# A block's decay gates: tanh quotient to exponential, and its mask rows from VectorE to ScalarE

## The reference, cut to what matters

```python
# LRU: r, i from the convolved input xc, per channel
r = sigmoid(einsum(xb, wr) + br);  i = sigmoid(einsum(xb, wi) + bi)
log_a = -8.0 * r * softplus(-lam)
a = exp(log_a)
mult = sqrt(-expm1(2.0 * log_a))
bx = mult * i * xc
h[t] = a[t] * h[t-1] + bx[t]          # associative scan over time
return h * gelu(u_y)
# SSD, per head: a causal 256x256 mask of exp(cumulated decay differences) times C B^T, applied to x * dt
```

## Time and profile before

| | us |
|---|---|
| median of 3 runs | 2155.76 (2155.23 to 2159.41) |
| span of the profiled execution (the page gives no other time of it) | 2165.0 |
| busy in that span: PE / DVE / ACT / POOL | 1581.4 / 754.1 / 575.8 / 613.3 |
| the head loop, from the first `ssd_y` to the first matmul of the LRU's output layer | 1424.46 to 1507.34 |

### The profile page before, as it was taken

How to read it: one execution, slowest core, us unless ns; L and a number is a source line. 1 busy time by engine, 2 the same in 40 slices (tenths; PEclk the granted TensorE clock), 3 DMA queues, 4 the chain that set the end, 5 groups by cost and what they waited for, 6 DMA issues and landing times.

```text
span 2165.0 us, 25359 instructions
## 1 busy us (share of the span) xinstructions
PE 1581.4 (73%) x10341; PEld 1063.6 (49%) x10341; DVE 754.1 (35%) x989; ACT 575.8 (27%) x973; POOL 613.3 (28%) x252
## 2 busy tenths in 40 slices
PE   4969786665555656666556669687879787889897
PEld 2758642111111111111111259676769777878797
DVE  3225420000000000000000079889739885176333
ACT  4324420000000000000000044553644344444453
POOL 1144300000000000000000049543738556755473
PEclk8989877778888778777887779899979888998898
DMA  9455569999999999999999925222424333443330
GB/s 390 144 192 227 233 241 417 418 419 418 417 417 417 417 417 417 418 419 419 418 417 417 420 89 186 102 102 79 156 78 165 146 117 114 159 146 107 117 117 20
DMA packets 88740, 570.06 MB, mean 263 GB/s; under 512 B 4576, under 2 KB 10720, under 8 KB 44512
## 3 DMA queue, kind: packets, MB, share of 16 engines
q1 hardware_dynamic: 81440, 556.81, 64.2%
q10 hardware_dynamic: 7232, 12.29, 2.1%
HBM read 564.89 MB, written 4.19 MB: 263 GB/s over the span
## 4 chain that ended last, share of the span: by engine, by line
DMA 38%; PE 29%; DVE 25%; ACT 3%; issue 2%; DVEq 1%; another core or an unknown queue 1%; ACTq 0%; POOL 0%; SPq 0%
PE bank L1376 28%; DMA ring<-in_w_down 13%; DMA ring<-in_w_up 12%; DMA ring<-in_w_gate 12%; DVE work L157 4%; DVE work L810 4%; DVE work L806 3%; DVE work L155 1%; DMA ring<-in_dense 1%; ACT work L1692 1%; DVE work L728 1%; DMA ring<-in_w_ada 1%; DVE rstd L1928 1%; DVE work L1932 1%; ACT weights_high_rounded L1692 1%
## 5 line engine op out<-in xcount | busy, mean ns | idle before, releaser
L1357 POOL TENSOR_TENSOR ring_rounded<-ring,weights_high_rounded 128x1024 fp32r<-128x1024 f32 x244 | 608.2, 2505 | 1507.9 <-ACT weights_high_rounded L1692 1507.2
L1376 PE MATMUL bank<-ring,work 128*32 128x512 f32 x3008 | 490.7, 785 | 335.6 <-DMA ring<-in_w_up 129.8
L1692 ACT ACTIVATE work<-bank 128x256 f32<-128x256 f32 (+3 forms) x312 | 135.6, 441 | 1218.1 <-PE bank L1376 863.7
L1376 PEld LDWEIGHTS bank<-ring,work 128*32 128x32 f32 x3008 | 93.8, 127 | 698.7 <-DMA ring<-in_w_up 212.1
L1692 ACT ACTIVATE weights_high_rounded<-ring 128x1024 fp32r<-128x1024 f32 x244 | 255.9, 1052 | 34.1 <-PE bank L1376 22.1
L1376 PE MATMUL bank<-h_high_rounded,weights_high_rounded 128*128 128x256 f32 x1296 | 208.1, 302 | 56.6 <-ACT weights_high_rounded L1692 38.0
L2140 DVE TENSOR_TENSOR work<-work,bank 128x512 f32<-128x512 f32 x16 | 11.0, 688 | 602.4 <-PE bank L1376 602.4
L1376 PEld LDWEIGHTS bank<-h_high_rounded,weights_high_rounded 128*128 128x128 f32 x1296 | 177.7, 199 | 76.3 <-issue 40.7
L1376 PE MATMUL bank<-h_normed_rounded,weights_high_rounded 128*128 128x256 f32 x1296 | 186.7, 289 | 0.0
L1376 PE MATMUL bank<-h_high_rounded,ring_rounded 128*128 128x256 f32 x1296 | 182.4, 285 | 2.7 <-POOL ring_rounded L1357 2.7
L1376 PE MATMUL bank<-work_rounded,weights_high_rounded 128*128 128x256 f32 x1088 | 162.2, 300 | 29.0 <-ACT work_rounded L1692 20.3
(11 more groups left out here) (230 smaller groups left out, 1363.2 us busy)
## 6 DMA issues: line engine op xcount, KB each, us to landing
ring<-in_w_down SPq DMA_DIRECT2D x64, 2048.0 KB, 16.8
ring<-in_w_gate SPq DMA_DIRECT2D x63, 2048.0 KB, 16.6
ring<-in_w_up SPq DMA_DIRECT2D x61, 2048.0 KB, 16.5
ring<-in_dense SPq DMA_DIRECT2D x60, 2048.0 KB, 7.7
ring<-in_w_ada SPq DMA_DIRECT2D x12, 2048.0 KB, 20.5
work<-in_w_up SPq DMA_DIRECT2D x3, 1024.0 KB, 13.6
bias_diagonals<-work ACTq DMA_DIRECT2D x2, 1532.0 KB
ring<-in_dense SPq DMA_DIRECT2D x2, 1024.0 KB, 18.8
```

The lines of the kernel that those rows point to most:

```text
L1357: nc.gpsimd.tensor_tensor(as_r(w), w, w_high[:, buffer, :], ALU.subtract).then_inc(s.w_low, 1)
L1376: return nc.tensor.matmul(o, lhsT, rhs, start=start, stop=stop)
L1692: return nc.scalar.activation(o, i, f, **kw)
```

## The change: an exponential for the LRU's decay, mask rows on ACT

1. The decay a is no longer (1 + tanh) / (1 - tanh). ACT writes Tanh into `XC` (free once i * xc is made) and then Exp into `TH`, with the factor -8 in the new `LAMT`. `lru_input` is gone from DVE; `lru_scan` multiplies by (1 + a) in the instruction that added 1 before. Sqrt takes its minus sign from the activation's scale, so DVE's L737 is gone.
2. The eight products i * xc are made on DVE while the sigmoids come out, each after its own `ri_sig`, and ACT waits for all of them before Tanh.
3. The masked decay rows are written by ACT (`Identity` with a per-partition scale), three before the loop and then one in each head between `weight_high` and `decay(h+2)`. `LMASK` has three buffers; the third is the old `LRU_T`.

```diff
@@ tensor_block2
-                bank, lm = B[4 + h % 2], LMASK[:, h % 2, :]
+                bank, lm = B[4 + h % 2], LMASK[h % 3]
@@ scalar_block2
+            def mask_decay(h):
+                if h >= 3:
+                    act.wait_ge(s.bc_mm, h - 2)
+                fn(LMASK[h % 3], LCUM, ACT.Identity, scale=con("head_rows")[:, h:h + 1]).then_inc(s.lmask_ready, 1)
...
             act.wait_ge(s.ri_sig, KT)
+            act.wait_ge(s.cs_ready, 1)
+            mask_decay(0), mask_decay(1), mask_decay(2)
+            act.wait_ge(s.ixc_ready, 1)
             for k in range(KT):
-                last = fn(TH[:, k, :], TH[:, k, :], ACT.Tanh, scale=LAMC[:, k:k + 1])
+                fn(XC[:, k, :], TH[:, k, :], ACT.Tanh, scale=LAMC[:, k:k + 1])
+            for k in range(KT):
+                last = fn(TH[:, k, :], TH[:, k, :], ACT.Exp, scale=LAMT[:, k:k + 1])
             last.then_inc(s.th_ready, 1)
...
-            act.wait_ge(s.lru_neg, 1)
-            fn(tiles(0, 8), tiles(0, 8), ACT.Sqrt).then_inc(s.lru_root, 1)
+            act.wait_ge(s.th_ready, 1)
+            fn(tiles(0, 8), tiles(0, 8), ACT.Sqrt, scale=-1.0).then_inc(s.lru_root, 1)
...
                     copy2(38 + h, RAW[:, 38 + h, :])
+                if h + 3 < SSM_H:
+                    mask_decay(h + 3)
                 if h + 2 < SSM_H:
                     decay(h + 2)
@@ vector_block2
+            v.tensor_scalar(LAMT, LAMC, -8.0, None, ALU.mult)
             v.tensor_scalar(LAMC, LAMC, -4.0, None, ALU.mult).then_inc(s.lam_ready, 1)
+
+            for k in range(KT):
+                i = tiles(I_OF[k], 1)
+                dve.wait_ge(s.ri_sig, k + 1)
+                last = v.tensor_tensor(i, i, XC[:, k, :], ALU.mult)
+            last.then_inc(s.ixc_ready, 1)
...
-            for h in range(2):
-                v.tensor_scalar(LMASK[:, h, :], LCUM, con("head_rows")[:, h:h + 1], None, ALU.mult).then_inc(s.lmask_ready, 1)
...
-                link(v.scalar_tensor_tensor(out=th, in0=th, scalar=1.0, in1=LRU_T, op0=ALU.add, op1=ALU.mult))
+                link(v.scalar_tensor_tensor(out=i, in0=th, scalar=1.0, in1=i, op0=ALU.add, op1=ALU.mult))
...
-            dve.wait_ge(s.th_ready, 1)
-            dve.wait_ge(s.ri_sig, KT)
-            for k in range(KT):
-                i = tiles(I_OF[k], 1)
-                last = v.tensor_tensor(i, i, XC[:, k, :], ALU.mult)
-            link(last)
-            v.tensor_scalar(tiles(0, 8), tiles(13, 8), -4.0, None, ALU.mult).then_inc(s.lru_neg, 1)
             segments(0)
-            mask_decay(2)
             segments(1)
...
                 if h + 2 < SSM_H:
                     segments(h + 2)
-                if h + 3 < SSM_H:
-                    mask_decay(h + 3)
-                if h % 2 == 0:
-                    lru_input(h // 2)
-                else:
+                if h % 2:
                     lru_scan(h // 2).then_inc(s.act_full, 1)
```

More of the change, by code:

```diff
@@ L95 @@
 lmask_ready seg_ready bc_mm xdt_ready m_ready ya_pair ssd_y ya_sq ya_sum w_high x_ready dt_in dt_soft xbc_conv
-lam_ready th_ready ly_gelu lru_neg lru_root seg_exp z_silu g_sig ya_gated ya_inv ya_rstd conv_step ffn_gelu
+lam_ready ixc_ready th_ready ly_gelu lru_root seg_exp z_silu g_sig ya_gated ya_inv ya_rstd conv_step ffn_gelu
 act_full act_high a_exp late_in lam_soft act_low bias_in lg_sb lg_mm lg_ready pt_sb pt_tr ao_mm gl_mm kp_ready
@@ L331, in program @@
         SEG = [tiles(71, 3)[:, 0:3 * P], tiles(71, 3)[:, 3 * P:6 * P], tiles(61, 2)[:, 0:3 * P]]
-        LMASK = tiles3(74, 2)
+        LMASK = [tiles(74, 1), tiles(75, 1), tiles(12, 1)]
         I_OF = (8, 9, 10, 11, 76, 77, 78, 79)
@@ L335, in program @@
         DTT = small(112, 32).rearrange("p (t h) -> p t h", t=TT)
-        LRU_T = tiles(12, 1)
         PA, PB, MO2 = tiles3(29, 8), tiles3(21, 8), tiles3(13, 8)
@@ L699, in segments @@
                                 ALU.subtract, ALU.min).then_inc(s.seg_ready, 1)
[L701 to L706, removed]
             def lru_scan(k):
@@ L711, in lru_scan @@
                 if k == 0:
+                    dve.wait_ge(s.th_ready, 1)
                     dve.wait_ge(s.lru_root, 1)
                     dve.wait_ge(s.ly_gelu, 1)
-                link(v.scalar_tensor_tensor(out=th, in0=th, scalar=1.0, in1=LRU_T, op0=ALU.add, op1=ALU.mult))
+                link(v.scalar_tensor_tensor(out=i, in0=th, scalar=1.0, in1=i, op0=ALU.add, op1=ALU.mult))
                 link(v.tensor_tensor(i, i, XC[:, k, :], ALU.mult))
@@ L723, in pair_out @@
                                        in1=B[6 + n % 2][:, 0:SEQ], op0=ALU.mult, op1=ALU.add).then_inc(s.ya_pair, 1)
-            def mask_decay(h):
-                dve.wait_ge(s.bc_mm, h - 1)
-                v.tensor_scalar(LMASK[:, h % 2, :], LCUM, con("head_rows")[:, h:h + 1], None, ALU.mult).then_inc(s.lmask_ready, 1)
-            dve.wait_ge(s.th_ready, 1)
-            dve.wait_ge(s.ri_sig, KT)
-            for k in range(KT):
-                i = tiles(I_OF[k], 1)
-                last = v.tensor_tensor(i, i, XC[:, k, :], ALU.mult)
-            link(last)
-            v.tensor_scalar(tiles(0, 8), tiles(13, 8), -4.0, None, ALU.mult).then_inc(s.lru_neg, 1)
             segments(0)
-            mask_decay(2)
             segments(1)
```

## The result

| | before | after |
|---|---|---|
| median of 4 runs each, us | 2155.49 (2153.04 to 2159.41) | 2173.28 (2172.02 to 2175.21) |
| span of the profiled execution, us | 2165.0 | 2170.2 |

The ratio is 1.0086, 95% interval 1.0070 to 1.0103: slower. The forecast was 2174.8 us.

A forecast was written before the change was run, and what follows sets the result against it. It took DVE, held by POOL through their shared port, to bound the head loop, with PE waiting for its product. Terms +3.8, +2.5, -1.3, +15.0 and -1.0 gave +19.0 us: 2174.8 us, range 2153 to 2181 (0.8).

The forecast's parts named there:

- ACT ahead of the loop: Before the head loop: added mask rows, exponentials and a table load on ACT delay PE's first head output by 3.8 us.
- First fall of the clock: Around the first head output: PE idle 5 us or more, so the granted clock falls, costing 2.5 us (1.6 to 3.4).
- Heads 1 to 3: First pair, heads 1 and 2: product ahead of POOL, PE 1.0 us late, 9.8 us against 11.1, so -1.3.
- Five pairs: Head 3 to head 13: POOL holds the even product, PE waits 3.6 us, clock falls; 14.0 us a pair, +15.0 in all.
- Tail: From head 13's output to the LRU's output layer: 11.0 us instead of 12.06, so -1.0.
- Sum: All terms from the start of the loop to its tail added: +19.0 us, giving 2174.8 us against the median of 2155.76.
- Everything behind the loop shifts with it: After the head loop: all work is released by PE and shifts with it; DMA, share 0.00, has weights in time.
- the product slips ahead of POOL: Rival, in the loop: even product starts before POOL, pairs of 10.6 us, sum -1.1, 2154.7 us; chance 0.14.
- The clock holds: Rival, in the loop: PE's waits do not lower the clock, pairs of 12.4 us, sum +9.5, 2165.3 us; chance 0.12.
- PE becomes the bound: Rival, in the loop: POOL does not hold DVE's two-input instructions, product ready in time, sum -13.0, 2142.8 us; chance 0.09.
- the 0.05 for a time above 2181: Case of longer low-clock stretches than counted, giving a time above 2181 us; chance 0.05.

The follow-up runs named there:

- e6: The changed kernel with ACT's eight LRU decay exponentials moved behind the exponentials of heads 0 and 1; 2171.63 us, ratio 1.0068 to the kernel before.
- e1: The changed kernel with ACT's mask row ahead of weight_high instead of behind it in even heads; 2156.37 us, ratio 1.0003 to the kernel before.
- e2b: The changed kernel with five filler matmuls on PE in even heads from 4 on, before the product wait; 2168.01 us, ratio 1.0049 to before.
- e2: The changed kernel with ten filler matmuls on PE in even heads from 4 on, before the product wait; 2178.36 us, ratio 1.0095 to before.
- e5: The changed kernel with the even head's product and the pair's sum ahead of the odd head's LRU chain on DVE; 2152.89 us, ratio 0.9978 to before.
- e7: The changed kernel with the edits of e5 and e6 together; 2143.42 us, ratio 0.9931 to the kernel before.
- e8: The kernel before (quotient, mask rows on DVE) with only e5's new order on DVE; 2177.34 us, ratio 1.0085 to the kernel before.
- e4: The kernel before with only the mask rows moved to ACT and three buffers, quotient kept; 2159.47 us, ratio 1.0017 to the kernel before.

## Why the prediction was right

- *ACT ahead of the loop, +3.8.* Measured +3.76 (+17.26 to +21.02). The table load cost 1.29 up to the next instruction, as the row of before had said (1.30). The Trainium skill, ScalarE: Activation LUTs, "What ACT_TABLE_LOAD costs", gives 1.38 us more for a drain; the trace shows none behind the load. e6 shows that the eight Exp and their load are what the first output paid for: without them there it came 4.3 earlier.
- *First fall of the clock, +2.5.* Clock 0.50 from 1418.06 for 6.83 us; head 0 to head 1 took 6.97 against 4.44, +2.5. That the size fits so well is luck: 2.5 was the middle of two bounds, 1.6 and 3.4, and not worked out.
- *Heads 1 to 3, -1.3.* Measured 9.88 against 11.14: -1.3.
- *Five pairs, +15.0.* Measured 71.65 against 55.24: +16.4. The mechanism is as worked out: POOL 0.29 us ahead of the product (worked out: 0.24), PE's wait 3.60, e1 turns it off by letting the product be first. The term was mis-sized by 0.3 a pair. By e2b a pair without a fall is 12.55, not 12.4, and a fall costs 1.8 in the mean, not 1.6; one of the five lasted 6.83 us instead of 3.41.
- *Tail, -1.0.* Measured 10.03 against 12.06: -2.0. The last two outputs, at the low clock and back to back, took 1.95 (1515.90 to 1517.85) and not 2 x 1.5.
- *Sum +19.0* against 19.4 in the stage, and 17.8 between the medians. The pairs (1.4 too little) and the tail (1.0 too much) partly cancel, so the sum fits better than its terms. "Everything behind the loop shifts with it" holds roughly, not exactly. The DMA share of 0.00 in the earlier trace rows is that of the tail alone; from the first output to the LRU's output layer it was 0.28 before and 0.24 in after, and no engine's wait there was put down to a DMA. Two windows from the LRU's output layer to the end, first of before, then of after:

```profile
1507.34:2165.00 657.66, 559.12 (x4075) 531.39 (x4074) 379.62 (x465) 306.48 (x514) 377.09 (x151) 0.90 0.33 119
```

```profile
1517.85:2170.20 652.35, 552.30 (x4075) 524.03 (x4074) 380.51 (x465) 306.45 (x514) 379.01 (x151) 0.91 0.33 120
```

The same instructions took 5.3 us less, PE alone 6.8 less, at a slightly higher granted clock. Over the twelve profiles this stretch lies between 652.4 and 658.8 with no order by the length of the loop (e2: 657.3, e5: 658.4, e7: 653.6), so I read it as a spread of single executions, not as time given back; that is argued, not shown: each kernel has one profile.

Of the rivals, *the product slips ahead of POOL* is what e1 made: pairs of 10.93 with one fall of the clock, 10.6 without, and 2156.4 (it was given 2154.7). *The clock holds* is what e2b made: pairs of 12.55, ratio 1.0049, where +9.5 us (1.0044) was worked out. *PE becomes the bound* failed on L726, 2.5 us in every odd head; e5 and e7 come within 0.4 us of PE's 8.87 a pair by another way. The chances have a slip: the 0.05 for a time above 2181 is slower too, so the chance of slower comes to 0.81, not 0.76.

The price of a mask row on ACT, 0.41 us, was taken from eight Tanh in 3.30, and it held as what a row adds: three took 1.31 (1.23 was worked out), and in the loop the next instruction starts 0.40 us behind a row's start. The 0.50 us that a group's mean gives for one (ACT in after, below) is its length from start to end, of which 0.1 lies under the next instruction; the Tanh and Exp have 0.495 by the same count.

```profile
L1685 ACT ACTIVATE work<-work,consts 128x256 f32<-128x256 f32 x12 | 6.0, 498 | 0.0
```

## What to carry to other kernels

What a removal is worth is read from where the instruction that others wait for comes to stand, not from the busy time removed. Here 5.5 us of DVE's busy time per pair went (two rows of 1.9 and a reciprocal of 1.75), of which 3.1 was waiting for POOL, since a row that is not held runs in 0.34. The pair grew by 3.3, because the product that PE waits for came to stand 0.3 us behind POOL's start instead of 0.15 ahead of it. After such a removal, write the instruction that the other engine waits for at the earliest place its inputs allow, ahead of chains whose result is needed only later, and try the order again with the new arithmetic; an order found good for the one can be bad for the other (e8). A wait of PE that recurs is paid twice where the granted clock falls with it (here 1.8 us a pair).

## What the runs showed of the hardware

- Between POOL's subtraction and a DVE instruction with two inputs in SBUF, the one that starts first runs and the other waits, and hundredths decide. With POOL 0.29 us ahead (after, L740), 0.36 ahead in the gap behind L725 (after, L726) or 0.06 ahead (e8, L706), DVE's instruction ends only 0.28 to 0.42 us behind POOL's end. A product 0.11 us ahead of POOL (e1) runs in 0.55 and stretches POOL by 0.35 (2.69 against 2.34). Between 1390 and 1530 us of the twelve profiles, a DVE instruction of this kind that the trace has 0.04 or 0.05 us behind POOL's start still ran first in eleven of twelve cases (e5: L725 at 1456.21 in 0.41 us, POOL from 1456.17 in 2.73), and from 0.06 to 0.17 us behind it was held every time. DVE instructions with an input in PSUM keep their 0.47 us under POOL (after, L733 at 1441.36).
- PE idle for 3.6 us in each pair brought the granted clock to 0.50 in every pair (after). Idle for 1.19 us with 2.4 us of filler behind it (e2b) never did in the loop, idle for 1.68 did once in the loop (e1), idle for 2.33 in front of the first output did not (e6), and in e4 the clock fell behind waits of 1.78 and 2.73 with four matmuls between them.
